# An S5 scan stage: unread wide products among narrow ones, table blocks placed by ScalarE, copies shared by three engines

## What is computed

```python
def s5_mixer(h, ...):                    # 64 groups of 16 channels, 64 complex states each
    u = (h @ w_in).reshape(bsz, seq, 64, 16)
    abar = exp(dt * (ar + i*ai))         # in real and imaginary parts
    bb = f * b                           # f from abar and a
    bu = einsum('blgh,gph->blgp', u, bb)
    st = associative_scan(_complex_scan_op, (abar, bu))   # along the 256 tokens
    y = einsum(st_re, c_re) - einsum(st_im, c_im) + d_skip * u
    y = gelu(y)
    z = y * sigmoid(y @ w_glu + b_glu)
    return z @ w_out
```

## Time and profile before

| | |
|---|---|
| median of 3 runs | 3721.84 us (3721.25 to 3723.36) |
| profiled execution, its own time | 3720.3 us |
| its span in the profile | 3718.5 us |
| busy in the span: PE / PEld / DVE / ACT / POOL | 3353.2 / 3003.2 / 2362.0 / 1710.2 / 1163.4 us |
| mean granted clock of TensorE | 0.933 of full speed |

### The profile page before, as it was taken

How to read it: one execution, slowest core, us unless ns; L and a number is a source line. 1 busy time by engine, 2 the same in 40 slices (tenths; PEclk the granted TensorE clock), 3 DMA queues, 4 the chain that set the end, 5 groups by cost and what they waited for, 6 DMA issues and landing times. The chain is left out here.

```text
span 3718.5 us, 64947 instructions
## 1 busy us (share of the span) xinstructions
PE 3353.2 (90%) x21028; PEld 3003.2 (81%) x21028; DVE 2362.0 (64%) x4662; ACT 1710.2 (46%) x3458; POOL 1163.4 (31%) x1087
## 2 busy tenths in 40 slices
PE   7989899999289996897899999997889889999997
PEld 7879798999179884797688999987569867899996
DVE  8954487786868544587844555554367895455555
ACT  4443644444054442454744444454245474444443
POOL 3242021120702100057863333310003886333332
PEclk9995899998589997999999999998589999999999
DMA  5530487783058551553055555554024405555554
GB/s 181 169 125 1 136 313 286 295 317 107 0 187 323 191 177 45 162 163 111 30 187 172 186 182 187 184 170 146 7 80 148 158 6 166 173 183 187 183 187 146
DMA packets 163124, 590.85 MB, mean 159 GB/s; under 512 B 18596, under 2 KB 19236, under 8 KB 162728
## 3 DMA queue, kind: packets, MB, share of 16 engines
q1 hardware_dynamic: 143824, 521.95, 42.4%
q10 hardware_dynamic: 19160, 67.18, 4.7%
HBM read 588.00 MB, written 1.06 MB: 158 GB/s over the span
## 5 line engine op out<-in xcount | busy, mean ns | idle before, releaser
L318 PEld LDWEIGHTS ps<-hT,parts 128*128 128x128 f32 x12864 | 1592.9, 193 | 106.9 <-DVE parts L142 43.1
L318 PE MATMUL ps<-hT,parts 128*128 128x256 f32 x12864 | 1612.8, 285 | 71.3 <-DVE parts L142 28.3
L142 DVE TENSOR_TENSOR parts<-ring,parts 128x512 fp32r<-128x512 f32 x1786 | 1181.6, 697 | 606.8 <-ACT parts L137 598.0
L137 ACT ACTIVATE parts<-ring 128x512 fp32r<-128x512 f32 x1930 | 1157.4, 628 | 601.4 <-PE ps L318 570.8
L318 PE MATMUL ps<-parts,gatedT 128*128 128x512 f32 x4128 | 1010.7, 398 | 10.3 <-DVE parts L142 10.3
L318 PEld LDWEIGHTS ps<-parts,gatedT 128*128 128x128 f32 x4128 | 765.1, 190 | 177.3 <-POOL gatedT L1048 7.9
L1184 POOL TENSOR_TENSOR gatedT<-acted,iota 128x256 fp32r<-128x256 f32 x264 | 179.1, 678 | 1430.1 <-PE ps L318 1172.9
L142 POOL TENSOR_TENSOR parts<-ring,parts 128x512 fp32r<-128x512 f32 x144 | 213.8, 1507 | 587.3 <-ACT parts L137 586.1
L1155 ACT ACTIVATE acted<-ps 128x256 f32<-128x256 f32 x264 | 101.7, 385 | 598.6 <-PE ps L318 598.5
L1187 POOL TENSOR_TENSOR gatedT<-acted,gatedT 128x256 fp32r<-128x256 f32 x264 | 314.0, 1189 | 20.7
L1168 DVE TENSOR_TENSOR acted<-acted,big 128x256 f32<-128x256 f32 x176 | 74.9, 426 | 359.3 <-ACT acted L1155 359.3
(11 more groups left out here) (333 smaller groups left out, 2270.0 us busy)
## 6 DMA issues: line engine op xcount, KB each, us to landing
ring<-wts SPq DMA_DIRECT2D x965, 512.0 KB, 3.5
big<-mod_wts ACTq DMA_DIRECT2D x112, 512.0 KB, 4.7
big<-rows SPq DMA_DIRECT2D x15, 512.0 KB, 5.2
big<-mod_bias ACTq DMA_DIRECT2D x14, 512.0 KB, 4.2
big<-mod_rows SPq DMA_DIRECT2D x4, 512.0 KB, 4.6
big<-peer_keys SPq DMA_DIRECT2D x2, 1024.0 KB, 4.9
x<-x_in SPq DMA_DIRECT2D x1, 1024.0 KB, 4.9
big<-s_bc ACTq DMA_DIRECT2D x4, 256.0 KB, 3.3
```

Of the source, the lines that this page charges most:

```text
L137: act.activation(self.part(n, half, 0), self.raw(n, half), ACT.Copy).then_inc(self.hi_done, 1)
L142: v.tensor_tensor(self.part(n, half, 1), self.raw(n, half), self.part(n, half, 0).bitcast(F32), ALU.subtract).then_inc(self.lo_done, 1)
L318: last = pe.matmul(out, a(x), b(y), start=start and x + y == 0, stop=stop and x == 1)
```

## The change

Three things are edited.

1. `ScanTables`: `blocks` becomes `product`. VectorE writes the two sums over all 128 partitions into a buffer (`sums`, two in turn) and signals `summed`; ScalarE copies them to their places in four pieces of 64 partitions (`place`), two pieces behind each of two tiles, and signals `placed`, for which VectorE waits before it writes a buffer again. `times_step` takes real and imaginary part together (four operations instead of six) and no longer has a tile of its own. The two `cx` copies per half go to ScalarE.
2. First S5 stage: the last 16 of the 64 copies into chunk order are taken from GpSimd; ScalarE and VectorE do one each behind each of their eight puts.
3. Scan stage: after every third product TensorE makes one of 512 columns from weight parts that lie in SBUF, into PSUM bank 3, which nobody reads (`keep_clock`). The ends so have three banks in place of four, and are issued three groups ahead in place of four.

```diff
-        def blocks(src, factor, dst, slot, negative):
+        def product(b, src, factor, before, negative):
+            yield
+            if before:
+                times_step(factor, before)
             re, im = src
...
             yield
             st.wait()
-            for h in range(2):
-                ps, cs = slice(64 * h, 64 * h + 64), slice(32 * slot + GH * h, 32 * slot + GH * h + GH)
-                st.done(v.tensor_tensor(dst[0][ps, :, cs], w[0][ps], w[1][ps], ALU.subtract))
-                if negative:
-                    st.done(v.scalar_tensor_tensor(dst[1][ps, :, cs], w[2][ps], -1.0, w[3][ps], ALU.mult, ALU.subtract))
-                else:
-                    st.done(v.tensor_tensor(dst[1][ps, :, cs], w[2][ps], w[3][ps], ALU.add))
-                yield
+            if b >= 2:
+                v.wait_ge(s["placed"], 4 * (b - 1))
+            st.done(v.tensor_tensor(out[0], w[0], w[1], ALU.subtract))
+            if negative:
+                last = v.scalar_tensor_tensor(out[1], w[2], -1.0, w[3], ALU.mult, ALU.subtract)
+            else:
+                last = v.tensor_tensor(out[1], w[2], w[3], ALU.add)
+            st.wait()
+            last.then_inc(s["summed"], 1)
...
+    def place(self, act, s, b, part):
+        if part == 0:
+            act.wait_ge(s["summed"], b + 1)
+            if b == STEP:
+                act.wait_ge(s["zeroed"], 2)
+        for dst, at, h in self.places[b]:
+            ps = slice(64 * h, 64 * h + 64)
+            act.activation(dst[part][ps, :, at:at + GH], self.sums[b % 2][part][ps], ACT.Copy).then_inc(s["placed"], 1)
...
+        def moves(c):
+            return [(to[32 * r:32 * r + 32, c:c + 2, j, :], at.u[32 * j:32 * j + 32, c:c + 2, r::STEP]) for r in range(STEP) for j in range(4)]
...
                 act.activation(*put(n), ACT.Copy).then_inc(s["g_act"], 1)
+                act.activation(*moves(KC - 2)[n], ACT.Copy)
...
                 v.tensor_copy(*put(n)).then_inc(s["g_dve"], 1)
+                v.tensor_copy(*moves(KC - 2)[n])
...
-            for c in range(0, KC, 2):
+            for c in range(0, KC - 2, 2):
...
+            unread = k.w.part(first, 0, 0)
+            count = 0
+
+            def keep_clock(products=1):
+                nonlocal count
+                count += products
+                if count >= 3:
+                    count = 0
+                    pe.matmul(k.ps[:, 3, :], unread[:, 0:P], unread, start=True, stop=True)
+
             def ends(g):
-                if g >= 4:
-                    pe.wait_ge(s["v_read"], 2 * (g - 3))
+                if g >= 3:
+                    pe.wait_ge(s["v_read"], 2 * (g - 2))
...
+                        if (m, n) != (3, 1):
+                            keep_clock()
...
+                        if (m, n) != (15, 1):
+                            keep_clock()
...
+                    if m < 3:
+                        keep_clock(3)
...
             ends(2)
-            ends(3)
             within(1)
             for g in range(groups):
-                if g + 4 < groups:
-                    ends(g + 4)
+                if g + 3 < groups:
+                    ends(g + 3)
                 outputs(g)
```

More of the change, by code:

```diff
@@ L1234 @@
 class ScanTables:
-    sems = "bc_in dt_exp mag_exp red sines zeroed table"
+    sems = "bc_in dt_exp mag_exp red sines zeroed table summed placed"
     def __init__(self, k):
@@ L1243, in __init__ @@
         self.terms = [big[:, 6144 + 512 * n:6656 + 512 * n].rearrange("p (s h) -> p s h", s=ST) for n in range(4)]
-        self.prod = big[:, 8192:9216].rearrange("p (s q) -> p s q", s=ST)
+        self.sums = [[big[:, 8192 + 1024 * b + 512 * n:8704 + 1024 * b + 512 * n].rearrange("p (s h) -> p s h", s=ST) for n in range(2)]
+                     for b in range(2)]
+        self.prod = big[:, 6144:7168].rearrange("p (s q) -> p s q", s=ST)
+        blocks_of = lambda dst, slot: [(dst, slot + GH * h, h) for h in range(2)]
+        self.places = ([blocks_of(self.at.turned, 32 * (STEP - 1 - n)) for n in range(STEP)] +
+                       [blocks_of(self.at.outof, 32 * n) for n in range(STEP)])
         self.pieces = None
@@ L1256, in scalar @@
             act.activation(par[:, DT, :], par[:, DT, :], ACT.Exp).then_inc(s["dt_exp"], 1)
-        elif n == 1:
+        for b in range(2 * STEP):
+            if n in (self.FIRST + 3 * b + 5, self.FIRST + 3 * b + 6):
+                self.place(act, s, b, n - self.FIRST - 3 * b - 5)
+        if n == 3:
+            act.wait_ge(s["bc_in"], 64)
+            for h in range(2):
+                ps, cs = slice(64 * h, 64 * h + 64), slice(GH * h, GH * h + GH)
+                act.activation(self.at.cx[0][ps, :, cs], self.bc_in[2][ps], ACT.Copy)
+                act.activation(self.at.cx[1][ps, :, cs], self.bc_in[3][ps], ACT.Copy, scale=-1.0)
+        if n == 1:
             act.wait_ge(s["red"], 1)
@@ L1332, in double_angle @@
             st.link(v.tensor_scalar(q(o + 1), q(T0), 2.0, None, ALU.mult))
-        def blocks(src, factor, dst, slot, negative):
+        def product(b, src, factor, before, negative):
+            yield
+            if before:
+                times_step(factor, before)
             re, im = src
             fr, fi = (bc(q(f).unsqueeze(2), [P, ST, GH]) for f in (factor, factor + 1))
-            w = self.terms
+            w, out = self.terms, self.sums[b % 2]
             st.wait()
@@ L1372, in work @@
         for n in range(STEP):
-            if n:
-                times_step(PWR + 2 * n, PWR + 2 * n - 2)
-                yield
-            yield from blocks((c_re, c_im), PWR + 2 * n, at.outof, n, True)
+            yield from product(STEP + n, self.bc_in[2:4], PWR + 2 * n, PWR + 2 * n - 2 if n else None, True)
+        yield
+        tt(T0, S5_MAG, S5_MAG, ALU.mult)
+        st.link(v.tensor_tensor(at.mag4, q(T0), q(T0), ALU.mult))
         double_angle(POW, COS, SIN)
@@ L1534, in by_cos @@
                     v.wait_ge(s["y_ready"], g - 2)
-                v.tensor_tensor(two(at.work[g % 3]), two(k.ps[:, g % 4, :]), angle(at.cos, g), ALU.mult).then_inc(s["v_read"], 1)
+                v.tensor_tensor(two(at.work[g % 3]), two(k.ps[:, g % 3, :]), angle(at.cos, g), ALU.mult).then_inc(s["v_read"], 1)
             by_cos(0)
```

41 lines of the change are left out of this document (15 added, 26 removed).

## The result

| | before | changed |
|---|---|---|
| median | 3722.5 us (3721.3 to 3723.4, 4 runs) | 3748.8 us (3747.7 to 3753.1, 4 runs) |
| profiled execution, its own time | 3720.3 us | 3747.7 us |
| its span | 3718.5 us | 3745.9 us |
| mean granted clock | 0.933 | 0.928 |

The ratio is 1.0073, 95% interval 1.0060 to 1.0085: the change is slower by 26 us. The forecast of 3684 us was wrong, and so was the range, by 0.8 us at its high end. What happened is the second rival, the clock that falls in the gap and is not brought back.

What follows compares the result with a forecast made beforehand. The scan stage was taken as bound by TensorE at the low clock. From 3720.3 us, tables +4, entry -6.3 and scan stage -34.0 gave 3684 us, range 3675 to 3748, if the clock is high for nearly the whole stage.

Steps and rivals of the forecast that it cites:

- the second rival: Scan stage: the clock falls in the gap and unread products do not bring it back; 3741.5 us, chance 0.36.
- Does the clock hold?: Scan stage: leaned to the mix of narrow and unread products climbing to and holding 2.4 GHz, like the attention stretch.
- The gap: Before the scan stage: TensorE restarts 3.9 us after the transposes; long enough that the clock can be lost.
- The sign that I named for being wrong: Scan-stage windows in the profile after: granted clock reads 0.50 and the stage lasts 120 us or more.
- Returns at once, as at 388: Scan-stage rival: clock falls at the entry, returns after 5.4 us; 3686.7 us, chance 0.52 together with the forecast.
- Unread products at 1.2 GHz: Scan stage at the low clock: the 62 unread products add 20.5 to 26.7 us, 23.5 taken.
- Scan stage at 2.4 GHz: Real products 51.3 us plus unread ones 14.9 make 66.2 us, a saving of 34.0.
- They stay under TensorE, by little: Scan stage at 2.4 GHz: VectorE's 4.85 us and ScalarE's 4.6 plus some 0.5 per group stay below TensorE's 5.7.
- Entry: Before the scan stage: GpSimd's 48 copies instead of 64 save 6.3 us, between 6.9 and 5.0.
- Tables: First FFN: the changed scan tables make VectorE late, costing +4 us, from -1.5 to +8.
- The sum: Whole kernel: 3720.3 + 4 - 6.3 - 34.0 gives 3684 us; the low-clock rival's sum is 3741.5, chance 0.36.
- The high end of the range: Whole kernel: low-clock rival's 3741.5 + 3.2 (wide products at full price) + 4 (tables), given as 3748 us.

Runs made afterwards that it cites:

- e9: Changed kernel with a denser filling of about 143 unread products in the scan stage, the gap before it left unfilled; 3783.1 us, ratio 1.0154.
- e7: Changed kernel with 12 unread products in the gap and denser filling, one behind every single product in the 32-column blocks; 3709.0 us, ratio 0.9953.
- e2: Changed kernel with 12 more unread products in the gap before the scan stage; 3732.1 us, ratio 1.0042.
- e4: Changed kernel with 16 unread products in a row at the head of the scan stage, gap unfilled; median 3744.1 us, ratio 1.0033.
- e3: Changed kernel with 12 unread products in the gap but none in the scan stage; 3718.1 us, ratio 0.9989.
- e5: Changed kernel with 12 unread products in the gap and one behind every second product in the 32-column blocks; 3700.0 us, ratio 0.9944.
- e10: Kernel before with only the shared chunk copies and three banks of ends, no unread products, old tables; 3712.9 us, ratio 0.9969.
- e8: Kernel before with only the changed kernel's ScanTables class; 3727.2 us, ratio 1.0003.
- b8: b6 with 12 more unread products, a second one for each output tile in the last three output groups; 3687.3 us, ratio 0.9897.
- b1: Changed kernel with old tables, copies shared further, 6 unread products in the gap, one in two in 32-column blocks and outputs; 3690.5 us, ratio 0.9907.
- b5: b1 with an unread product behind every product in the 32-column blocks and one in three in the outputs; 3695.3 us, ratio 0.9927.
- b6: b5 with the unread products of the 32-column blocks cut from 512 to 384 columns; 3692.7 us, ratio 0.9917.
- b7: b5 with 12 more unread products, a second one for each output tile in the last three output groups; 3694.3 us, ratio 0.9918.

## Why the prediction was wrong, point by point

**Does the clock hold?** This is the step that failed, in two places. First, I took the attention stretch at 2712 us, which "climbs and holds", for the row nearest to the mix. It does climb: the clock comes back at 2711.3 us, amid products of 128 and 256 columns, and the changed kernel's low stretch there is 10.3 us longer. But the mix is not such work. Behind a gap the change needed a mix that brings the clock back, and e9 shows that this one doesn't even when it is far denser: its 143 fillers leave 1.2 GHz for 161 us, while with the gap filled the same filling never loses 2.4 GHz (e7). Second, even as a question of holding the lean was wrong at one in three: with the gap filled, e2 fell 21 us into the stage. That "the wide product is K=128 and one is in each 0.9 us" was an argument from the look of the mix, with no row of such a mix at either clock. The rows had no case in which products of 32 to 64 columns brought the clock back, and two in which narrow work stayed low (the scan stage and 2636 us); by them the rival with 0.36 deserved more than the forecast's 0.52.

**The gap.** I wrote that TensorE "still had 2.4 GHz" 3.9 us into the gap and that 3.9 is long. The gap was 3.69 us, and in the window above the clock reads 1.00 up to 275.6; it fell just behind the restart, as at 1957. In e9 it fell at 273.8 us, 0.8 us before the restart. This half of the reading was right, and it should have carried the forecast. The sign that I named for being wrong (0.50, 120 us or more) is what came.

**Returns at once, as at 388.** e4 bears out that dense wide work raises it (0.50 for 2.9 us from its first product on). The mix isn't such work.

**Unread products at 1.2 GHz.** 20.5 to 26.7 us, 23.5 taken; measured 26.1. The 0.1 us of each that was to lie beside the next load didn't show: the period of 1.71 us is the plain sum. At 2.4 GHz the same holds: in e2 the unread products stand 0.90 us apart (294.63 and 295.53 us) with three products between them, 0.69 for six narrow records of 0.115 and 0.21 for the unread one.

**Scan stage at 2.4 GHz.** Narrow records at 0.115 us (3.69 us for 32 in e3) stand against 0.11 forecast, unread ones at 0.21 against 0.24. But 66.2 us would not have come about: in e5, with ten more unread products (2.1 us), the stage took 76.0 us, 11.1 of them low. "They stay under TensorE, by little" held only while ends stand beside the outputs; the last three groups went by ScalarE's 4.6 us, and the wait of 1.4 us was followed by a fall. Even without a lost clock at the start, 3684 was some 8 us short, more than half of it this late fall.

**Entry.** -6.3 forecast, -6.9 measured in the changed kernel and -6.8 in e10. The step was right, the copies on the two engines cost nothing of it, and the gain of 5.0 that stood for VectorE and GpSimd meeting did not come. As profiled, ScalarE's copy lasted 0.42 to 0.45 us, not 0.3, and its pairs still ended before GpSimd's last copy. VectorE's took 0.27.

**Tables.** +4 forecast; 2.4 us in the changed kernel's profile, of which 1.4 are left when its late start is taken off, and 1.2 in e8. The range of -1.5 to +8 holds all of them. The rounds of 9.07 us are inside the 8.6 to 9.6 named. The four terms of VectorE's three tiles add up to 8.4 us, not 8.5, which changes nothing.

**The sum.** The rival's own sum was 3741.5; with the measured terms it is 3720.3 + 2.4 - 6.9 + 26.1 = 3741.9. The profiled execution took 5.8 us more, in code that the change doesn't touch, 5.1 of them where the clock came back late in sparse attention, and no term stood for that. The high end of the range was made of the terms alone, and mis-added: 3741.5 + 3.2 + 4 is 3748.7, not 3748. The median of 3748.8 is above either, but that it lies so close to the end is luck, as the terms were smaller than that end took them and the rest came from elsewhere.

## What to carry to other kernels

Ask two questions of any filler meant to keep TensorE's clock: is there a gap in front of it that loses the clock before it begins, and is there a row that shows work like it, in its own widths, *raising* the clock and not only keeping it. If the first product behind a gap starts low, each filler is paid at the slow rate and buys nothing. Fill the gap first: here 6 wide unread products that wait for no other engine's copies, 1.6 us, were enough; make the filling densest where the products are narrowest; and recount each engine's time per group at the high clock, as the engine that was second before becomes the one waited for where the filling work runs out. Try the plain part alone, too: sharing the copies by itself came out 10 us faster, 6.8 of them seen in the trace.

## What the runs showed of the hardware that was not expected

The same stream of instructions ran for 161 us at 1.2 GHz when it was entered there (e9) and all through at 2.4 GHz when entered at that level (e7). The Trainium skill (TensorE: Matmul & The Clock Gate, Part 1) has it that activity releases the throttle; in e9 being busy, 161.2 of 161.2 us, was not enough. The Trainium skill (TensorE: Matmul & The Clock Gate, HAM oscillation) describes a kernel that waits between bursts and begins each burst cold; here a gap of 3.69 us in front of the scan agrees, and the gap of some 0.9 us in e2, e3 and b8 did not cost the clock.

Near the edge the outcome differs from one execution of a kernel to the next: e4 gave 3700.6 and 3756.2 us, b1 3688.0 and 3750.0. A median over few executions says little there; a count of lost ones says more. And late in the stage, among one-in-three outputs, a wait of 1.42 or 1.43 us was followed by a fall within 0.3 to 2.0 us in all three profiles that had it (e5, b5, b6), while a wait of 0.5 us was followed by none in six. Whether the wait or the thinner work on both sides of it weighs more isn't separated by b7, which removed both.
